# Hybrid encoder layer: queries and keys projected with the weights stationary, and rotated across partitions

## The reference

```python
h = rmsnorm(x, norm_mix)
rq, rk, rv, rg, aq, ak, av, gate_logits = split(h @ w_in)
# retention: 4 heads, keys of 128, values of 256; forward and backward decay
q, k = rotate(rq, ret_inv), rotate(rk, ret_inv) * 128 ** -0.5
ret  = retention(q, k, v, fwd) + retention(reversed, bwd)
# attention: 3 groups (window, dilation) of 8 heads of 64, merged by their softmax weights
qa, ka = rotate(aq, att_inv) * 64 ** -0.5, rotate(ak, att_inv)
att  = merge(banded_attention(qa, ka, va) for each group)
x = x + (gates0 * (silu(rg) * norm(ret)) @ w_ret_out + gates1 * att @ w_att_out) @ w_out
x = x + expert_choice_ffn(rmsnorm(x))      # 16 experts of 2048, SwiGLU, 128 tokens each
y = rmsnorm(x)

def rotate(x, inv_freq):                   # x1, x2: the two halves of a head's channels
    return concatenate([x1 * cos - x2 * sin, x2 * cos + x1 * sin])
```

## Time and profile before

| | us |
|---|---|
| median of 3 runs | 2442.28 (2441.58 to 2443.16) |
| the profiled execution, its own time | 2441.73 |
| its span | 2439.9 |
| TensorE busy | 2412.3 (99%) |
| VectorE, ScalarE, GpSimd busy | 1623.7 (67%), 1371.8 (56%), 333.9 (14%) |
| mean granted TensorE clock | 0.996 of full |

### The profile page before, as it was taken

One profiled execution on the slowest core, in us unless ns is written; L12 is line 12 of the kernel. 1 busy time (PEld: TensorE's weight loads), 2 busy tenths in 40 slices (PEclk: granted clock), 3 DMA queues, 4 the chain that ended last, 5 costly groups with the idle time before them and its releaser, 6 DMA issues.

```text
span 2439.9 us, 36720 instructions
## 1 busy us (share of the span) xinstructions
PE 2412.3 (99%) x12864; PEld 2083.9 (85%) x12864; DVE 1623.7 (67%) x2119; ACT 1371.8 (56%) x1673; POOL 333.9 (14%) x287
## 2 busy tenths in 40 slices
PE   8999999999999999999998999999999999999998
PEld 7998989888898999988886888888888888888886
DVE  5455544544544554445345888888888888888897
ACT  4434444533434444345232777777777777777776
POOL 1313222100023223230002000000000000000000
PEclk9999999999999999999999999999999999999999
DMA  5212121224522212122236999999999999999998
GB/s 188 96 64 95 51 90 64 78 86 151 211 65 96 73 69 98 47 86 73 100 138 226 401 390 386 382 380 389 393 389 384 385 383 386 381 384 387 384 385 307
DMA packets 142321, 556.36 MB, mean 228 GB/s; under 512 B 10032, under 2 KB 17840, under 8 KB 134320
## 3 DMA queue, kind: packets, MB, share of 16 engines
q1 hardware_dynamic: 135200, 529.80, 57.2%
q0 software_dynamic: 7056, 25.69, 3.5%
HBM read 532.39 MB, written 23.07 MB: 228 GB/s over the span
## 4 chain that ended last, share of the span: by engine, by line
PE 96%; DVE 2%; ACT 1%; issue 1%; POOL 0%; DMA 0%; DVEq 0%; POOLq 0%; ACTq 0%; SPq 0%
PE bank L1327 43%; PE bank L987 20%; PE bank L1032 13%; PE bank L964 6%; PE bank L1007 4%; PE bank L1048 3%; PE bank L1160 2%; PE bank L1373 2%; PE bank L1141 1%; PE bank L1084 1%; PE bank L1121 1%; PE bank L1088 1%; PE bank L1127 1%; PE bank L1218 1%; POOL w_lo L803 0%
## 5 line engine op out<-in xcount | busy, mean ns | idle before, releaser
L2391 DVE TENSOR_TENSOR m_lo<-m_raw,m_hi 128x2048 fp32r<-128x2048 f32 x380 | 867.5, 2291 | 120.9 <-ACT m_hi L1787 117.5
L1787 ACT ACTIVATE m_hi<-m_raw 128x2048 fp32r<-128x2048 f32 x382 | 733.6, 1921 | 259.8 <-PE bank L1327 256.6
L987 PE MATMUL bank<-w_hi,h_hi 128*128 128x384 f32 (+1 forms) x1024 | 341.5, 333 | 1.7 <-DVE h_lo L2232 0.9
L987 PE MATMUL bank<-w_hi,h_lo 128*128 128x384 f32 (+1 forms) x1024 | 330.0, 322 | 0.0
L987 PE MATMUL bank<-w_lo,h_hi 128*128 128x384 f32 (+1 forms) x1024 | 329.4, 322 | 0.0
L1327 PE MATMUL bank<-m_hi,xs_hi 128*128 128x512 f32 x1032 | 321.0, 392 | 0.0
L1327 PE MATMUL bank<-m_hi,xs_lo 128*128 128x512 f32 x1032 | 317.9, 389 | 0.0
L1327 PE MATMUL bank<-m_lo,xs_hi 128*128 128x512 f32 x1032 | 317.8, 389 | 0.0
L1924 DVE TENSOR_TENSOR w_lo<-w_raw,w_hi 128x1152 fp32r<-128x1152 f32 (+4 forms) x110 | 140.9, 1282 | 212.3 <-ACT w_hi L1447 212.3
L1327 PEld LDWEIGHTS bank<-m_lo,xs_hi 128*128 128x128 f32 x1032 | 193.7, 188 | 40.5
L1327 PEld LDWEIGHTS bank<-m_hi,xs_lo 128*128 128x128 f32 x1032 | 193.7, 188 | 40.4
(11 more groups left out here) (275 smaller groups left out, 3769.1 us busy)
## 6 DMA issues: line engine op xcount, KB each, us to landing
m_raw<-in_w_exp_gate SPq DMA_DIRECT2D x128, 1024.0 KB, 8.8
m_raw<-in_w_exp_up SPq DMA_DIRECT2D x128, 1024.0 KB, 7.6
m_raw<-in_w_exp_down SPq DMA_DIRECT2D x128, 1024.0 KB, 7.3
w_raw<-in_w_b SPq DMA_DIRECT2D x22, 1536.0 KB, 6.7
w_raw<-in_w_a SPq DMA_DIRECT2D x24, 1024.0 KB, 5.2
w_raw<-in_w_c SPq DMA_DIRECT2D x24, 1024.0 KB, 4.8
w_raw<-in_w_d SPq DMA_DIRECT2D x8, 1024.0 KB, 6.1
xt<-in_x SPq DMA_DIRECT2D x8, 512.0 KB, 8.3
```

The lines of the kernel that those rows point to most:

```text
L987: last = pe.matmul(ps_proj[:, proj.slot, 0:cols], a[:, c, tokens], v[:, c, :], start=c == n == 0, stop=c == chunks - 1 and n == 2)
L1787: act.activation(m_hi[slot.slot][:, :, :], m_raw[raw.slot][:, :, :], ACT.Copy)\
L2391: dve.tensor_tensor(m_lo[slot.slot][:, :, :], m_raw[raw.slot][:, :, :], m_hi[slot.slot][:, :, :].bitcast(F32), ALU.subtract)\
```

## The change

Queries and keys are now projected *turned*: the weights of 128 channels are stationary and all 512 tokens move, so that the result has channels on the partitions and tokens in the columns, the form that R's transposes made before. A new step **J u g** does this (`project_pair`, 24 matmuls of 512 columns: 8 channel chunks, three passes). An attention block has six J (q and k of three groups; each holds two heads of 64), a head part two (q, k). The attention's values keep the old way, all three groups side by side, 384 columns wide (P 2 i, four per block). The weight units are cut differently for this: one unit holds the q of three groups, one the k, one the v, each fetched with three transfers of 512-byte pieces in place of one of whole rows.

Rotation: the two halves that are mixed now lie on different partitions. ScalarE copies the halves crosswise out of PSUM into `crossed` (`cross`: four copies of 32 partitions x 512 for attention, two of 64 x 512 for retention); VectorE multiplies `crossed` by the signed sines, in place, and the bank by the cosines into `rot`, which frees the bank; GpSimd adds the two (128 x 512). For attention groups 1 and 2 the sum goes straight to `qk_t`. R shrinks to one copy of 128 x 512 by ScalarE and one subtraction by VectorE, for group 0 and for retention only.

The tables `rope_r` and `rope_a` are [128, 2, 512] now; `rope_r` is loaded once a batch. `dist` is one signed table in place of two. `v_a` is one tile, written at the end of the attention part, and `shift_values` waits for that. The opening projects values first, then the six J.

```diff
-    order = "P S0 P P S1 P S2 P P S3 P P I P P T0 U0 P T1 U1 P T2 U2"
+    order = "J S0 J S1 P S2 P S3 P P I P P T0 U0 P R0 T1 U1 P R1 T2 U2"
...
+def attention_schedule():
+    extra = {0: (("T", 3), ("U", 3)), 1: (("V",), ("G", 2)), 2: (("K", 0), ("K", 1)),
+             3: (("h", 0), ("K", 2), ("K", 3), ("l", 0)), 4: (("h", 1), ("v",), ("l", 1), ("w",)),
+             6: (("O", 0), ("O", 1)), 7: (("O", 2), ("O", 3)), 9: (("A", 0), ("A", 1))}
+    out = turned_schedule(extra)
+    for i in range(NT):
+        out.append(("P", 2, i))
...
+def turned_schedule(extra):
+    for n in range(2 * NG):
+        u, g = divmod(n, NG)
+        if g == 0:
+            out += [("u",), ("W", 0), ("W", 1), ("W", 2)]
+        out.append(("J", u, g))
+        out.extend(extra.get(n, ()))
+        if behind:
+            out.append(behind.pop(0))
+        if g == 0:
+            behind.append(("R", u, 0))
...
+            def load_pair(h, u):
+                sp.wait_ge(s_wlo[w.slot], START + w.lap)
+                for g in range(NG):
+                    sp.dma_start(by_group(w_raw[w.slot][:, :])[:, g, :, :],
+                                 w_b[h, g].rearrange("p (c n) -> p c n", c=KC)[:, :, natural(u)])\
+                        .then_inc(s_wraw[w.slot], 16)
...
-            def add_rotation():
-                pool.wait_ge(s_rope_x, turn.n(1))
-                pool.tensor_tensor(rot1[turn.slot][:, :], rot1[turn.slot][:, :], rot2[turn.slot][:, :],
+            def add_rotation(u, g, opening=0):
+                tile_read(pool, proj)
+                pool.tensor_tensor(rotated(u, g, turn), rot[turn.slot][:, :], crossed[turn.slot][:, :],
                                    ALU.add).then_inc(s_rope, 1)
...
+            def project_pair(wh, wl):
+                pe.wait_ge(s_proj_free[proj.slot], START + proj.lap)
+                for c in range(KC):
+                    for n, (v, a) in enumerate(((wh, h_hi), (wl, h_hi), (wh, h_lo))):
+                        last = pe.matmul(ps_proj[:, proj.slot, :], v[:, c, :], a[:, c, :],
+                                         start=c == n == 0, stop=c == KC - 1 and n == 2)
+                last.then_inc(s_proj, 1)
...
-                        for j in range(2):
-                            last = pe.transpose(ps_out[:, turned.slot, natural(j)], rot1[rope.slot][:, natural(j)],
-                                                ident[:, :])
-                        transposes([rot1[rope.slot][:, 0:P], rot1[rope.slot][:, P:2 * P]])
+                    t["turned" if arg[0] is None else "pair"].k += 1
...
+            def cross(u, i):
+                turn, width = t["turn"], DH // 2 if u is not None else RDK // 2
+                act.wait_ge(s_proj, START + proj.n(1))
+                act.wait_ge(s_rope, START + turn.n(-1))
+                for at in range(0, P, 2 * width):
+                    low, high = slice(at, at + width), slice(at + width, at + 2 * width)
+                    act.activation(crossed[turn.slot][low, :], ps_proj[high, proj.slot, :], ACT.Copy)
+                    last = act.activation(crossed[turn.slot][high, :], ps_proj[low, proj.slot, :], ACT.Copy)
+                last.then_inc(s_crossed, 1)
...
-            def rotate(table, i, groups):
-                dve.tensor_tensor(a, wide, table[:, i, 0, :].unsqueeze(1).to_broadcast([P, 2 * groups, half]),
-                dve.scalar_tensor_tensor(y2[:, :, 0, :], x[:, :, 1, :], -1.0, sin, ALU.mult, ALU.mult)
-                dve.tensor_tensor(y2[:, :, 1, :], x[:, :, 0, :], sin, ALU.mult).then_inc(s_rope_x, 1)
+            def rotate(u, i):
+                if turn.slot in rests:
+                    dve.wait_ge(*rests.pop(turn.slot))
+                dve.wait_ge(s_rope, START + turn.n(-1))
+                dve.wait_ge(s_crossed, turn.n(1))
+                dve.tensor_tensor(crossed[turn.slot][:, :], crossed[turn.slot][:, :], table[:, 1, :], ALU.mult)
+                dve.tensor_tensor(rot[turn.slot][:, :], ps_proj[:, proj.slot, :], table[:, 0, :], ALU.mult)\
+                    .then_inc(s_proj_free[proj.slot], 1)
```

More of the change, by code:

```diff
@@ L60 @@
 HALVES = ((0, 4), (4, 8))
[L61 to L66, removed]
+PER_HEAD = {"w": 6, "piece": 18, "proj": 16, "first": 1, "pair": 2, "turned": 2, "tr": 10, "sc": 12, "out": 6, "turn": 8, "ret": 1,
+            "score": 4, "step": 8, "link": 10, "cut": 1, "swap": 1, "raw0": 2 * NG + 1, "raw1": NG + 2}
+PER_COL = {"w": 4, "raw0": 2, "raw1": 2, "piece": 5, "half": 1, "proj": 4 * COLS, "mix": COLS, "hi": COLS}
+PER_BATCH = {"proj": 104, "mix": 8, "lo": 12}
+PAIR_TILES = 2 * NG + NT
+HEAD_TILES = 64
 GATES_DONE = HEAD_TILES + (4 * (D // NC) - 2) * COLS
@@ L945, in _ @@
         def _(pe):
-            t = some("w", "proj", "tr", "sc", "out", "rope", "ret", "step", "half", "turned", "cut", "swap")
+            t = some("w", "proj", "tr", "sc", "out", "turn", "ret", "step", "half", "turned", "pair", "cut", "swap")
             w, proj, tr, sc, outs = t["w"], t["proj"], t["tr"], t["sc"], t["out"]
@@ L1244, in run @@
                             project_values(u - 1, i)
                         else:
[L1246 to L1247 removed]
+                            project(natural(i))
                         if i == NT - 1:
+                            w.k += 1
+                    elif what == "J":
+                        if arg[1] == 0:
+                            unit_ready()
+                        if kind == "head":
+                            project_pair(*(a[w.slot][:, 0:KC * NA].rearrange("p (c n) -> p c n", n=NA)
+                                           [:, :, natural(arg[1])] for a in (w_hi, w_lo)))
+                        else:
+                            project_pair(*(by_group(a[w.slot][:, :])[:, arg[1], :, :] for a in (w_hi, w_lo)))
+                        if arg[1] == (1 if kind == "head" else NG - 1):
@@ L1435, in _, with loaded @@
         def _(act):
-            t = some("w", "proj", "tr", "sc", "out", "turn", "ret", "score", "mix", "hi", "first", "turned", "swap")
+            t = some("w", "proj", "tr", "sc", "out", "turn", "ret", "score", "mix", "hi", "first", "turned", "swap",
+                     "raw0", "raw1")
             w, proj, tr, sc, outs = t["w"], t["proj"], t["tr"], t["sc"], t["out"]
-            began = [0]
+            began, spun = [0], {}
+            def loaded(transfers):
+                raw = t[("raw0", "raw1")[w.slot]]
+                raw.k += transfers
+                act.wait_ge(s_wraw[w.slot], 16 * raw.n())
             def split_unit(size, part=None):
@@ L1640, in run @@
                             sizes.pop(0)
+                    elif what == "u":
+                        began[0] = proj.n()
+                    elif what == "J":
+                        cross(None if kind == "head" else arg[0], arg[1])
                     elif what == "P":
```

414 lines of the change are left out of this document (195 added, 219 removed).

## The result

The changed kernel takes 2417.55 us, median of 4 runs (2417.28 to 2419.16), against 2441.93 us (2440.99 to 2443.16) before: 24.4 us less, ratio 0.9902 [0.9886, 0.9918]. The forecast was 2407 us, so 10.5 us of the expected gain are missing. The profiled execution took 2417.55 us, its span 2415.7 us (before: 2441.73 and 2439.9), at a mean granted clock of 0.996 in both.

A forecast was written before the change was run, and what follows sets the result against it. TensorE was taken to bound the kernel, with 96% of the span. 2441.7 us - 37.9 for projections and transposes + 2 for waits + 0.5 for loads = 2406.3, median about 2407; range 2400 to 2424.

The forecast's parts named there:

- Projections: TensorE's projection matmuls: same columns, 768 fewer matmuls, each with some 13 ns fixed cost; gain 9.5 us.
- transposes: On TensorE, 128 pairs of transposes of `rot` go, 0.22 us each; gain 28.4 us.
- fixed part doesn't come back: Rival, 4%: stationary loads take the place of the fixed cost per matmul on TensorE; about 2415 us.
- The way out of the bank: Projection banks: crosswise copies 0.60 us, products 0.69 each; the bank returns in time, waits cost +2 us over eight blocks.
- (a): ScalarE behind G in the attention part: K 2 and K 3 find their banks free, no wait, margin 0.3 us.
- (b): Head part: S 2 needs S 1's two banks read and waits 0.2 to 0.3 us.
- (c): P 2 0 of the head part, waiting 0.22 us for GpSimd's last piece, stays within 0.3 us of before.
- Loads: Weight units in three transfers of 512-byte pieces: hidden except in the first opening, +0.5 us taken from 0 to +5.
- Port lock: Rival, 15% with similar holds: GpSimd's piece holds a VectorE SBUF operation in each head part, up to 1.84 us; 2421 us.
- TensorE's idle time within 5 us of before: Sign named in advance that, if seen over the whole kernel, would show the forecast right.
- Together 0.2 to 0.5 us per block: Sum of TensorE's waits at the three tightest places, over 8 blocks: +2 us.
- Slow crossing copies: Rival, 5%: ScalarE's crosswise copies take 1.12 us each, 2459 us; gain outweighed from about 1.0 us per copy.

The follow-up runs named there:

- the eighths: Each crosswise copy of ScalarE issued as eight pieces of 64 columns, against the changed kernel: 2459.13 us, ratio 1.0071 to the kernel before.
- the quarters: Each crosswise copy of ScalarE issued as four pieces of 128 columns, against the changed kernel: 2429.53 us, ratio 0.9948 to the kernel before.

## Why the prediction was right and where not

*Projections, -9.5 us, and transposes, -28.4 us:* right. Together -37.9, measured in busy time -37.7. Each was shown apart: a pair costs 0.21 to 0.24 us, a matmul's fixed part is what the distances say (0.1200 against 0.1195 read at 256 columns). The rival that the fixed part doesn't come back is out.

*The way out of the bank:* right, 0.59 us per copy, products of 0.69 where no GpSimd operation stands beside them (2.40 once), no wait at any J, also none in (a): K 2 starts at 137.85 without idle time, and only with copies of 0.76 us TensorE waits 0.77 us there, so the margin was a few tenths, as computed.

*(b), S 2:* right in six of eight blocks, 0.18 us where 0.2 to 0.3 were said. The 0.54 and 1.75 us behind the openings are 1.9 us more; by the rows shown above they come from holds, which no experiment tests.

*(c), P 2 0:* wrong. "within 0.3 us of before" holds for the chain (4.31 us against 4.32) but not for what GpSimd does to it. The hold of `stats` by the piece beside it adds some 0.9 us in each of eight blocks, 6.8 us in all.

*Loads, +0.5:* nothing is seen of them; TensorE's listed waits in the first opening are those of before, and 512 KB transfers land in 6.2 us where the earlier trace rows has 6.7 for three times as much.

*Port lock:* this rival, to which I gave 15%, holds beside the forecast's own mechanism, and the measured 2417.55 us lies nearer to its 2421 than to the forecast's 2407. The range held because the rival was in it; the 2407 was too low. The prediction's own sign, TensorE's idle time within 5 us of before, wasn't met either: it rose by 13.5 us. The rival named the mechanism and the chain (a `stats` of S 1 to S 3 behind a piece, the exponentials, P 2 0); I discounted it because I had followed the pieces of the first unit only (done at 5.9 us, first product at 6.9) and not those of the second, which S 2 and S 3 run beside, nor those of the attention part's first unit, beside `rqk_lo`. The holds cost 6.8 + 3.8 + 1.9 = 12.5 us; with 1.4 us for the rest of S 2 that is the 13.9 us of the three waits, where the prediction has 2. At P 2 0 the hold is less than the rival's 15 us because it lasts 0.9 us there, not a whole piece. The failed step is therefore "Together 0.2 to 0.5 us per block": it is 1.7 us per block (13.9 / 8). Shown: removing the held `stats` took P 2 0 from 1.08 to 0.25 us, moving either operation out of the other's way took the waits with it, and moving them into it cost 35 us.

*Slow crossing copies:* the copies weren't slow. The price of a single wait was nearly right. The break-even is about 0.86 us per copy, not 1.0, since the holds had used up part of the gain and the busy time grew with the waits.

The Trainium skill, SBUF — State Buffer, section Who interferes with whom, says that a VectorE operation with two SBUF inputs and a GpSimd one that reads SBUF exclude each other. The traces agree (`rqk_lo` 0.69 to 2.02 us, the head part's first product 0.69 to 2.40). `stats` and the scalings have one tensor input; that section lists TENSOR_SCALAR among the operations that can take both ports, and the traces show them held (0.17 to 1.05, 0.34 to 2.85 us) and holding: GpSimd's piece takes 4.49 us in place of 2.68 beside VectorE's scalings.

## What to carry to other kernels

When TensorE's list gets shorter, go through every operation from SBUF to SBUF on VectorE, the tiny ones too, and ask which GpSimd operation now stands beside it. Here `stats`, 4 elements in a partition, took up to 1.70 us, until the GpSimd operation had ended. The cure is order: put GpSimd's work where VectorE reads banks or where nobody waits for VectorE. And price a long wait of TensorE with what the clock takes after it: here 1.6 to 2.6 us behind each wait of 3.70 us, worked out from the granted clock of the 4 to 5 us that follow, or about half of the wait again.

## What I had not expected of the hardware

- The clock falls after short waits, but not after each. It fell behind six of six waits of 3.70 us (13.8 us more busy time over the kernel), behind four of six waits of 2.56 us and one of 2.59 in the eighths, and in the quarters behind their longest wait, 2.10 us (granted clock 0.72 over the next 6 us). In the six versions whose waits in a block are at most 1.3 us, a single one of 1.6 to 1.8 us apart, it fell behind none of them, and the busy time is 2372.0 to 2375.6 us. It isn't all clock: the quarters' busy time is 4.7 us over the changed kernel's, of which that stretch explains 1.7.
- A series of VectorE operations from SBUF to SBUF without gaps kept GpSimd out until it ended (the piece of 4.49 us). Where a piece began together with the second scaling, VectorE was held for a whole piece, twice running (2.85, 2.71 us).
- A copy between partition ranges on ScalarE costs what a plain one does: 591 ns for 32x512, 594 for 64x512, 599 for 128x512. Queued behind each other, 128 columns cost 0.191 us and 64 columns 0.123 us.
- Moving one tiny operation to the engine of its consumer gave back 4.4 of the 10.2 us of waits that it removed: ScalarE's copies came 0.7 us later, and the scores waited.
